# Gate and up projections of a decoder layer by Strassen's seven products over pairs of feed-forward tiles

## What is computed

```python
hf = rms_norm(x, g_pre_ffn)
ffn = (jax.nn.silu(hf @ w_gate) * (hf @ w_up)) @ w_down
return x + rms_norm(ffn, g_post_ffn)
```

## Time and profile before

| | |
|---|---|
| median of 3 runs | 1927.19 us (1925.48 to 1930.2) |
| profiled execution | 1931.76 us, of which the traced span is 1930.1 us |
| PE busy | 1808.7 us (94% of the span), 13317 matmuls |
| PEld busy | 1604.3 us (83%) |
| DVE, ACT, POOL busy | 910.1 us, 576.5 us, 241.9 us (47%, 30%, 13%) |
| DMA | 184.22 MB, mean 95 GB/s |

### The profile page before, as it was taken

The page is one execution under the profiler, slowest core; times in us unless marked ns, Lnnn a source line. Parts: engine busy times, 40 slices in busy tenths (PEclk is TensorE's granted clock), DMA queues, the critical chain, the costliest instruction groups (busy, mean ns, idle before and its releaser), DMA issues. The chain is left out here.

```text
span 1930.1 us, 34627 instructions
## 1 busy us (share of the span) xinstructions
PE 1808.7 (94%) x13317; PEld 1604.3 (83%) x13317; DVE 910.1 (47%) x1828; ACT 576.5 (30%) x1197; POOL 241.9 (13%) x547
## 2 busy tenths in 40 slices
PE   7889999899785999999998999999999999999998
PEld 6889999676463666667676889999999999999998
DVE  4423332125343776767775543333333332665655
ACT  4101010223232656565565640000000000344343
POOL 3000015400510322232221000000000000000000
PEclk9989999999996989999998999999999999999998
DMA  4434946745999012030201221111111110311112
GB/s 133 167 90 131 243 148 109 226 140 170 305 319 230 18 42 59 13 88 2 88 2 66 88 82 55 43 43 50 48 43 43 48 50 27 134 44 41 44 43 101
DMA packets 157263, 184.22 MB, mean 95 GB/s; under 512 B 23689, under 2 KB 120376, under 8 KB 157074
## 3 DMA queue, kind: packets, MB, share of 16 engines
q1 hardware_dynamic: 132658, 143.37, 24.5%
q0 software_dynamic: 11072, 30.78, 5.8%
q10 hardware_dynamic: 13408, 8.42, 2.0%
HBM read 152.30 MB, written 34.38 MB: 97 GB/s over the span
## 5 line engine op out<-in xcount | busy, mean ns | idle before, releaser
L183 PE MATMUL psum<-hf_hi,gu_hi 128*128 128x352 f32 x1056 | 341.1, 323 | 0.7 <-DVE gu_lo L2683 0.7
L184 PE MATMUL psum<-hf_lo,gu_hi 128*128 128x352 f32 x1056 | 338.8, 321 | 0.0
L185 PE MATMUL psum<-hf_hi,gu_lo 128*128 128x352 f32 x1056 | 338.6, 321 | 0.0
L183 PEld LDWEIGHTS psum<-hf_hi,gu_hi 128*128 128x128 f32 x1056 | 198.3, 188 | 1.0 <-DVE gu_lo L2683 0.9
L184 PEld LDWEIGHTS psum<-hf_lo,gu_hi 128*128 128x128 f32 x1056 | 198.6, 188 | 0.0
L185 PEld LDWEIGHTS psum<-hf_hi,gu_lo 128*128 128x128 f32 x1056 | 198.1, 188 | 0.0
L183 PE MATMUL psum<-x_hi,w_hi 128*128 128x352 f32 x528 | 173.0, 328 | 7.8 <-DVE w_lo L631 3.4
L183 PE MATMUL psum<-h_parts,down_hi 128*128 128x352 f32 x528 | 171.6, 325 | 8.6 <-ACT ffn_out L2630 5.5
L2014 ACT ACTIVATE probs<-psum,neg_max 128x640 f32<-128x640 f32 (+7 forms) x192 | 138.0, 719 | 119.9 <-DVE neg_max L2151 116.2
L184 PE MATMUL psum<-x_lo,w_hi 128*128 128x352 f32 x528 | 172.5, 327 | 0.0
L185 PE MATMUL psum<-x_hi,w_lo 128*128 128x352 f32 x528 | 172.4, 326 | 0.0
(11 more groups left out here) (377 smaller groups left out, 3169.9 us busy)
## 6 DMA issues: line engine op xcount, KB each, us to landing
fox_ring<-in_cache_fox_kv SPq DMA_DIRECT2D x128, 256.0 KB, 5.5
zT<-z_stage SPq DMA_DIRECT2D x22, 528.0 KB, 2.9
w_ring<-in_w_in POOLq DMA_DIRECT2D x22, 512.0 KB, 5.3
gu_ring<-in_w_ffn_gate SPq DMA_DIRECT2D x22, 512.0 KB, 3.8
gu_ring<-in_w_ffn_up SPq DMA_DIRECT2D x22, 512.0 KB, 3.9
down_ring<-in_w_ffn_down SPq DMA_DIRECT2D x44, 256.0 KB, 2.7
nsa_page<-in_cache_nsa_kv POOLq DMA_DIRECT2D x64, 128.0 KB, 6.4
out<-nat SPq DMA_DIRECT2D x12, 512.0 KB
```

The source lines that it names most:

```text
L183: nc.tensor.matmul(dst, w_hi, x_hi, start=start, stop=False)
L184: nc.tensor.matmul(dst, w_hi, x_lo, start=False, stop=False)
L185: return nc.tensor.matmul(dst, w_lo, x_hi, start=False, stop=stop)
```

## The change

The first SINGLE = 4 feed-forward tiles are made as before. The other 18 are made in 9 pairs. For each pair and each matrix (18 matrices m in all, even m gate, odd m up) the product of a [256 columns x 1024 depth] weight block with the [1024 depth x 1056 rows] of hf is cut into 2 x 2 blocks: two column tiles, two depth halves (4 tiles each), two row halves (NH = 528). Strassen's scheme in Winograd's form makes the four result blocks from seven block products instead of eight. A block product (`strassen(m, pos)`) is 2 banks of NQ = 264 rows x 4 depth tiles x 3 matmuls, 24 matmuls of 264 columns.

What comes with it:

- Row sums t1 to t4 of quarters of hf (`combine`, `rows_high`, `rows_low`), made once: 11 DVE operations over 4 x 528 elements, 4 ACT casts and 4 DVE subtractions of the same size.
- For each matrix: one load of 1 MB into `raw` (two slots), one multiplication by the gain over 8 x 256 elements, four sums S1 to S4 and seven casts (ACT) and subtractions (DVE) over 512 elements each.
- The seven products share 6 of the 8 PSUM banks. Later products are accumulated onto earlier ones after ACT has copied the intermediate (`snap`: p1, u1, p5); DVE adds the copies to the banks (`add_sums`: c11, c22, c12) and, for up, multiplies by the gate's SiLU (`times_gate`).
- h no longer fits in SBUF beside this. Tiles of 0 to 19 are stored to `h_dram` by DMAs that POOL issues and loaded back for the down projection, most of them while and after the last matrix is multiplied; tiles 20 and 21 stay in SBUF.
- The PSUM banks of the down projection are shifted, and tiles are placed anew in SBUF.

The core of the diff (order lists, placements and renamed buffers left out):

```diff
+def placed(nc, name, address, shape, dt=F32):
...
+SINGLE = 4
+PAIRS_OF_TILES = (FT - SINGLE) // 2
+MATRICES = 2 * PAIRS_OF_TILES
+NH = N // 2
+NQ = N // 4
+KH = KD // 2
...
+OPERANDS = ("A11", "A12", "S2", "S1", "S3", "S4", "A22")
...
+        def bank_at(m, pos):
+            return {1: 2, 3: 4, 5: 4}.get(pos, 6 * (m % 2))
...
-                with sp.Fori(0, FT - 1) as f:
...
+                for f in range(1, SINGLE):
                     for s in range(2):
-                        sp.wait_ge(gu_split[s], f + 1)
-                        sp.dma_start(gu_ring[:, s], GU[s][:, :, bass.ds(f * P + P, P)]).then_inc(gu_loaded[s], 16)
+                        sp.wait_ge(gu_split[s], f)
+                        sp.dma_start(gu_ring[:, s], GU[s][:, :, f * P:f * P + P]).then_inc(gu_loaded[s], 16)
+                    if f == 1:
+                        DV.wait(sp, ("lo", QT, 1))
+                        load_raw(0)
+                        load_raw(1)
+                for m in range(2, MATRICES):
+                    SV.wait(sp, ("lo", m - 2, 6))
+                    load_raw(m)
...
+            @block.gpsimd
+            def _(pool):
+                for f in range(SINGLE):
+                    pool.wait_ge(h_ready, f + 1)
+                    pool.dma_start(h_dram[f], single(f)[:, :]).then_inc(h_stored, 16)
+                pool.wait_ge(h_stored, 16 * SINGLE)
+                pool.dma_start(h_first[:, :, :], h_dram[0:2].rearrange("f p n -> p f n")).then_inc(h_loaded[0], 16)
+                for j in range(PAIRS_OF_TILES - 1):
+                    f = SINGLE + 2 * j
+                    SV.wait(pool, ("c21", 2 * j + 1))
+                    pool.dma_start(h_dram[f:f + 2].rearrange("f p n -> p f n"), stage[:, :, :]).then_inc(h_stored, 16)
...
+                pool.wait_ge(h_stored, stored(PAIRS_OF_TILES - 2))
+                for n in range(3):
+                    SP.wait(pool, (MATRICES - 1, 2 + n))
+                    pool.dma_start(h_mid[:, 4 * n:4 * n + 4, :], h_dram[3 + 4 * n:7 + 4 * n].rearrange("f p n -> p f n")).then_inc(h_loaded[2 + n], 16)
+                SP.wait(pool, (MATRICES - 1, 6))
+                pool.dma_start(h_late[:, :, :], h_dram[15:20].rearrange("f p n -> p f n")).then_inc(h_loaded[5], 16)
...
+                def strassen(m, pos):
+                    hi, lo = rows_at(pos)
+                    fresh = pos in (0, 1, 3)
+                    for b in range(2):
+                        tok = slice(NQ * b, NQ * b + NQ)
+                        for k in range(KH):
+                            last = product(nc, psum[:, bank_at(m, pos) + b, 0:NQ], op_hi[:, pos, k, :], op_lo[:, pos, k, :], hi[:, k, tok], lo[:, k, tok],
+                                           fresh and k == 0, k == KH - 1, not fresh)
+                    SP.done(last, (m, pos))
+
+                pe.wait_ge(silu_ready, SINGLE)
+                for m in range(MATRICES):
+                    SV.wait(pe, ("lo", m, 0))
...
+                    strassen(m, 0)
+                    SV.wait(pe, ("lo", m, 1))
+                    if m:
+                        SV.wait(pe, ("c11", m - 1))
+                    else:
+                        pe.wait_ge(h_ready, SINGLE)
+                    strassen(m, 1)
+                    SV.wait(pe, ("lo", m, 2))
+                    SA.wait(pe, ("p1", m))
+                    strassen(m, 2)
...
+                    SV.wait(pe, ("lo", m, 4))
+                    SA.wait(pe, ("u1", m))
+                    strassen(m, 4)
...
+                for m in range(MATRICES):
+                    is_gate, more = m % 2 == 0, m + 1 < MATRICES
+                    snap(m, "p1", 0, 0, "c11")
+                    if m == 0:
+                        rows_high(4)
+                    if more:
+                        weights_high(m + 1, 0)
+                    if is_gate:
+                        gate(m, "s11", "c11", 0, 0)
+                    if more:
+                        weights_high(m + 1, 1)
+                    snap(m, "u1", 1, 2, "c12")
...
+                combine(1)
+                for f in range(SINGLE - 1):
+                    dve.wait_ge(gu_done[0], f + 1)
+                    split_weights(f + 1, 0)
+                    gated(f)
+                    split_weights(f + 1, 1)
+                    if f == 0:
+                        combine(2)
+                        rows_low(1)
+                        rows_low(2)
+                    if f == min(1, SINGLE - 2):
+                        combine(3)
+                        rows_low(3)
+                dve.wait_ge(x1_stored, 16 * (QT + 1))
+                dve.wait_ge(h_stored, 16 * (SINGLE - 1))
+                gain_and_sums(0)
+                for pos in range(7):
+                    weights_low(0, pos)
+                gated(SINGLE - 1)
+                combine(4)
+                for m in range(MATRICES):
+                    up, more = m % 2 == 1, m + 1 < MATRICES
+                    if more:
+                        gain_and_sums(m + 1)
+                        weights_low(m + 1, 0)
+                    if m == 0:
+                        rows_low(4)
...
+                    add_sums(m, "c11", 1, 0, "p1", 0, 0)
```

More of the change, by code:

```diff
@@ L2257 @@
 FG = 2
-def gate_up_tiles(nc, ctx):
-    def sb(name, shape, dt=F32):
-        return ctx.enter_context(nc.sbuf_tensor(name, shape, dt))
[L2265 to L2276, removed]
+FFN_BASE = 20320
@@ new lines, in s_dve_order, with combined, early @@
+def s_dve_order():
+    def combined(x):
+        return [("part", x, n) for n in range(1 if x == 2 else 2)] + [("t", x)]
+    def early(m):
+        return [("gained", m)] + [("S", m, x) for x in (1, 2, 3, 4)]
+    names = combined(1) + combined(2) + [("t_lo", 1), ("t_lo", 2)] + combined(3) + [("t_lo", 3)]
+    names += early(0) + [("lo", 0, pos) for pos in range(7)] + combined(4)
+    for m in range(MATRICES):
+        up, more = m % 2 == 1, m + 1 < MATRICES
+        if more:
+            names += early(m + 1) + [("lo", m + 1, 0)]
+        if m == 0:
+            names.append(("t_lo", 4))
+        names.append(("c11", m))
+        if up:
+            names.append(("m11", m))
+        if more:
+            names += [("lo", m + 1, pos) for pos in (1, 2, 3)]
+        names.append(("c22", m))
+        if up:
+            names.append(("m22", m))
+        if more:
+            names.append(("lo", m + 1, 4))
+        names.append(("c12", m))
+        if up:
+            names += [("m12", m)]
+        if more:
+            names.append(("lo", m + 1, 5))
+        if up:
+            names += [("c21", m)]
+        if more:
+            names.append(("lo", m + 1, 6))
+    return names
@@ L2497, in _ @@
                         if g == 0 and q == 0:
[L2498 removed]
+                            SA.wait(pe, ("s21", MATRICES - 2))
+                            SV.wait(pe, ("c11", MATRICES - 1))
                         for c in range(2):
@@ L2606, in _, with rows_high, weights_high @@
[L2606 to L2610, removed]
+                def rows_high(x):
+                    SV.wait(act, ("t", x))
+                    SA.done(nc.scalar.copy(t_hi[x], t_sum[x]), ("t_hi", x))
+                def weights_high(m, pos):
+                    which = OPERANDS[pos]
+                    SV.wait(act, ("S", m, int(which[1])) if which[0] == "S" else ("gained", m))
+                    if m:
+                        SP.wait(act, (m - 1, pos))
+                    SA.done(nc.scalar.copy(op_hi[:, pos], weights(m, which)), ("hi", m, pos))
@@ new lines, in snap, with gate @@
+                def snap(m, name, n, pos, last):
+                    SP.wait(act, (m, pos))
+                    if m:
+                        SV.wait(act, (last, m - 1))
+                    SA.done(nc.scalar.copy(halves(snaps[:, n, :]), sums_at(m, pos)), (name, m))
+                def gate(m, name, sums_name, tile, c):
+                    SV.wait(act, (sums_name, m))
+                    part = silu[:, tile, NH * c:NH * c + NH]
+                    SA.done(nc.scalar.activation(part, part, ACT.Silu), (name, m))
@@ new lines, in weights_low, with add_sums @@
+                def weights_low(m, pos):
+                    SA.wait(dve, ("hi", m, pos))
+                    SV.done(nc.vector.tensor_tensor(op_lo[:, pos], weights(m, OPERANDS[pos]), op_hi[:, pos].bitcast(F32), ALU.subtract), ("lo", m, pos))
+                def add_sums(m, name, pos, n, snap_name, tile, c):
+                    dst = stage if m % 2 else silu
+                    SP.wait(dve, (m, pos))
+                    SA.wait(dve, (snap_name, m))
+                    SV.done(nc.vector.tensor_tensor(halves(dst[:, tile, NH * c:NH * c + NH]), sums_at(m, pos), halves(snaps[:, n, :]), ALU.add), (name, m))
```

330 lines of the change are left out of this document (283 added, 47 removed).

## The result

The changed kernel takes 1903.64 us (median of 4 runs, 1902.13 to 1907.55) against 1926.34 us of the kernel before beside it; ratio 0.9883, 95% interval 0.9865 to 0.9901, that is, by the ratio, 22.5 us less (19 to 26). The profiled execution took 1902.13 us, its span is 1900.4 us.

What follows compares the result with a forecast made beforehand. PE, busy 94% of the span, was taken to bound the kernel; -43.2 + 8.1 + 1.8 + 0.4 + 5.0 = -27.9 us from a median of 1927.2 gave 1899.3 us, range 1886 to 1916 (own range 1888 to 1914).

Steps and rivals of the forecast that it cites:

- Price of a matmul, and the products: Gate and up: 264-column matmuls at 122.0 ns; 3024 of them take 368.9 us instead of 412.1, -43.2 us.
- The rival that the weight load sets the pace: Gate and up: each load costs 159.0 ns, so the products take +68.7 us, 2011 us with the waits; chance 3%.
- DVE and ACT by their totals: Per matrix: DVE 12.0 us (14.8 for up), ACT 8.6, against PE's 20.5; neither becomes the bound.
- The steady state holds: Product 4 of each matrix: u1 copied at 10.3 us, wanted at 11.7; 1.4 us of slack, no wait.
- The wait of the first matrix: Product 4 of matrix 0: PE waits 8.1 us (6 to 12) behind DVE and ACT jobs, plus 1.8 for the clock.
- The clock as a rule of loops: Matrix loop, by the skill's rule: 1.8 us once if only the first matrix waits, 32 us if all 18 do.
- Covered work: Row sums and matrix 0's split fit where DVE idles and cost nothing; combine(1) 3 us short would cost 3 us once.
- Entry to the down projection: After the last matrix: +0.4 us for the first cast and +5 us (0 to 12) for late down weights.
- The first handover: Start of the down projection: the cast for h_parts1 takes 3.3 us against 2.9 of the first tile, +0.4 us.
- The wait for the down weights: Down projection, group 4: weights late because x1 and POOL's loads share bandwidth; +5 us, bounds 0 and 12.
- The working by equal shares: Down projection: two queues sharing 340 GB/s equally bring the weights at about 30 us; PE waits 8 us.
- The rival of POOL's slow queue: Loads of h for the down projection: at 99 GB/s PE loses 41 us, 1935 us in all; chance 5%.

Runs made afterwards that it cites:

- e5_widths: Changed kernel with the pairs' block products cut to widths from 264 to 160 columns, all weight loads kept; one execution of 1890.4 us, not comparable.
- e2_reorder: Changed kernel with matrix 1's gain and sums made earlier and, in matrix 0, c11, c22, u1 and p5 ahead of t4's split; 1895.39 us, ratio 0.9818.
- e6: Changed kernel with two further ScalarE copies (1.3 us more) ahead of the copy u1 of each matrix; one execution of 1906.95 us.
- e7: Changed kernel with five further ScalarE copies (3.15 us more) ahead of the copy u1 of each matrix; one execution of 1928.05 us.
- e4: Changed kernel with the last load of h issued only after x1 landed and group 4's weights were split; 1896.4 us, ratio 0.9829.

## Why the prediction was right, point by point

**Price of a matmul, and the products.** Forecast 122.0 ns, measured 121.4; the 18 matrices would need 18 x 20.39 = 367.1 us, 45.0 less than before, where 43.2 was forecast. The line through two widths and the floor from matmuls of one column were enough, and e5_widths shows why it was right to look at both: 264 lies 24 columns above the corner. The rival that the weight load sets the pace fell with it. The Trainium skill (Perfetto Trace Analysis, Identifying the Most-Contended Engine) names the busy share of weight loads, beside the share of the peak arithmetic, as the measure for TensorE; here PEld is busy 100% of a window both at 264 columns (340.00 of 340 us, above), where columns set the price, and at 352, so the share doesn't tell which of the two does.

**DVE and ACT by their totals.** Forecast 12.0 to 14.8 us of DVE for 20.5 of PE; measured 13.4 in matrix 1, an up matrix, for which 14.8 was forecast, and 12.3 in matrix 2, a gate matrix. Right within a tenth, a little too long.

**The steady state holds.** Forecast: u1 done at 10.3 us, wanted at 11.7. In the trace u1 starts 8.97 us into the matrix, as soon as product 2 is done, and lasts 0.60: the slack was 2.1 us, not 1.4. Right, and e6 and e7 bracket it.

**The wait of the first matrix.** Forecast 8.1 us plus 1.8 for the clock; measured 7.0 (7.1 by the distance of the matmuls) plus 1.7. Right in place, cause and size; e2_reorder showed the cause. The 1.8 itself was worked out low: ten matmuls in 4.4 us instead of 10 x 0.227 us are 2.1 us late, and nothing in the working said how much of the slow stretch the wait would hide.

**The clock as a rule of loops.** The waits of e7 in matrices 1 to 17 (1.0 us in each 21.7) never brought the clock down; those of 4.9, 6.9 and 7.1 us did, each before it was over. The Trainium skill (TensorE: Matmul & The Clock Gate, HAM oscillation) tells its rule, that a loop pays the clock again at each wait, of longer waits than those of e7. No run here has a loop with waits as long as the two that cost the clock, so the rule itself is neither met nor refuted.

**Covered work.** `combine(1)` to `combine(3)` and the splits of matrix 0 cost nothing: PE's only wait before matrix 0 is the 0.7 us that was there already.

**Entry to the down projection.** The first handover cost 0.64 - 0.16 = 0.5 us, forecast 0.4. The wait for the down weights is the term that was mis-sized: +5.0 forecast, measured 6.9 of wait plus 2.2 for the clock (16 matmuls in 4.8 us instead of 2.6). The working by equal shares had given 8 us with the weights at 30 us; they came at 28.5. I took 5 between that and the better cases, and forgot that a wait of this length also costs the clock, though the first wait had been charged for it. The windows of the wait's last 2 us and of these matmuls:

```profile
1630.40:1632.40 2.00, 0.00 (x0) 0.00 (x0) 1.98 (x3) 0.00 (x0) 0.00 (x0) 0.50 0.06 15
1632.40:1637.20 4.80, 4.77 (x16) 4.80 (x17) 2.08 (x3) 0.00 (x0) 0.00 (x0) 0.50 0.34 108
```

**The sum.** Forecast -27.9 us, measured -26.3 by stages and -22.5 (19 to 26) by medians, so the forecast lies outside the interval of the medians. That the stages come so near is in part luck: the products were 1.8 us better than forecast and the first wait with its clock 1.1 us, which made up for most of the 4.1 us by which the wait for the down weights was taken too short. Where the other 3.8 us between stages and medians come from is not shown; the stages ahead of gate and up vary by more than that from one profile to the next (1131.6 to 1139.2). The lower end of the prediction's own range doesn't follow from its errors: -6, -2 and -5 as independent errors give 8 us, so 1891 and not 1888. The rival of POOL's slow queue fell: its last load was not waited for by anyone, even 24 us late (e4).

## What to carry to other kernels

Fewer multiplications paid here because the matmuls stayed above 240 columns, where columns and not the weight load set their distance: price the new width from two known widths and a one-column matmul before rewriting anything. Behind such a change the losses sit at the two ends of the new stage: walk the order of every engine through the first iteration, and add up the bytes of all queues in flight when the stage ends. Charge each long wait with the clock it costs, and don't count on a shorter wait to give it back in proportion: one trace here shows it rise.

## What the runs showed of the hardware

- fp32r matmuls with a 128 x 128 weight load each, distance from one to the next at clock 1.00: 111.6 ns at 160 to 224 columns, 112.2 at 240, 115.0 at 248, 118.5 at 256, 121.4 at 264, against 159.0 at 352 and 226.8 at 512. Single-column matmuls with full loads stood 109 ns apart at clock 1.00, with loads of 32 columns 55 ns at clock 0.50.
- A wait shortened from 7.1 to 4.9 us raised the loss by the clock from 1.7 to 2.8 us: of the stretch at 0.50 the longer wait covered 3.2 us, the shorter one 0.8 us (one trace each).
- Two queues in flight on the same core, SP's and POOL's: the eight x1 loads took 15.3 us to landing instead of 7.7, with 400 to 420 GB/s in most slices of the stretch, and the weights behind them came 7.8 us later (28.5 us into the down projection instead of 20.7).
